# Norm sums: eight blocks of squares added on GpSimd, one matmul behind the low passes

## The reference, cut to what matters

```python
def rms_norm(x, g):
    y = x32 * lax.rsqrt(jnp.mean(x32 * x32, axis=-1, keepdims=True) + EPS)
    return (y * g.astype(jnp.float32)).astype(x.dtype)
...
        h = modulate(rms_norm(x, ln_ffn1[i]), sh1, sc1)
        x = x + 0.5 * g1[:, None, :] * swiglu(h, ffn1_wg[i], ffn1_wu[i], ffn1_wd[i])
        h = modulate(rms_norm(x, ln_mix[i]), sh2, sc2)
...
        x = x + g2[:, None, :] * mix
```

## Time and profile before

| what | value |
|---|---|
| runs shown | median 1736.61 us, 1735.37 to 1739.26, 3 runs |
| span of the profiled execution, first to last instruction | 1734.1 us |
| TensorE (PE) busy | 1708.0 us, 98% |
| VectorE (DVE) busy | 1412.9 us, 81% |
| ScalarE (ACT) busy | 908.4 us, 52% |
| GpSimd (POOL) busy | 435.0 us, 25% |
| mean granted clock of TensorE | 0.999 |

### The profile page before, as it was taken

The page is one execution under the profiler, slowest core; times in us unless marked ns, Lnnn a source line. Parts: engine busy times, 40 slices in busy tenths (PEclk is TensorE's granted clock), DMA queues, the critical chain, the costliest instruction groups (busy, mean ns, idle before and its releaser), DMA issues. The chain is left out here.

```text
span 1734.1 us, 36503 instructions
## 1 busy us (share of the span) xinstructions
PE 1708.0 (98%) x14039; PEld 1667.7 (96%) x14039; DVE 1412.9 (81%) x1924; ACT 908.4 (52%) x1274; POOL 435.0 (25%) x685
## 2 busy tenths in 40 slices
PE   7999999999999999999999999999999999999998
PEld 5999999999999999999999999999999998799998
DVE  6877898788778977898987799779988896788655
ACT  3443367764335533365634356667444567764444
POOL 6322321012223122321232224540322232401000
PEclk9999999999999999999999999999999999999999
DMA  9998858549887787867698865334988772257550
GB/s 338 356 359 279 294 178 280 166 158 321 304 304 242 276 302 270 302 212 272 229 314 305 302 199 191 115 132 156 322 297 293 230 199 83 78 199 251 184 176 25
DMA packets 261793, 411.45 MB, mean 237 GB/s; under 512 B 21950, under 2 KB 204414, under 8 KB 261560
## 3 DMA queue, kind: packets, MB, share of 16 engines
q1 hardware_dynamic: 224968, 290.67, 51.0%
q0 software_dynamic: 36720, 119.36, 19.4%
HBM read 408.90 MB, written 2.63 MB: 237 GB/s over the span
## 5 line engine op out<-in xcount | busy, mean ns | idle before, releaser
L2891 DVE TENSOR_TENSOR lo<-raw,hi 128x2048 fp32r<-128x2048 f32 (+2 forms) x251 | 565.6, 2256 | 162.4 <-ACT hi L2719 161.8
L2719 ACT CAST hi<-raw 128x2048 fp32r<-128x2048 f32 (+2 forms) x266 | 497.4, 1872 | 377.6 <-PE dacc L2388 189.4
L2386 PE MATMUL up<-operand_hi,hi 128*128 128x256 f32 x1952 | 553.1, 283 | 1.4 <-DVE lo L2891 1.4
L2387 PE MATMUL up<-operand_lo,hi 128*128 128x256 f32 x1952 | 552.3, 283 | 0.0
L2388 PE MATMUL up<-operand_hi,lo 128*128 128x256 f32 x1952 | 552.3, 283 | 0.0
L2163 POOL DMA_DIRECT2D ada<-in_ada_w_dram x448 | 267.3, 613 | 841.8 <-DVE ada_acc L2927 793.5
L2386 PEld LDWEIGHTS up<-operand_hi,hi 128*128 128x128 f32 x1952 | 374.4, 192 | 2.3 <-DVE lo L2891 2.0
L2388 PEld LDWEIGHTS up<-operand_hi,lo 128*128 128x128 f32 x1952 | 374.5, 192 | 0.0
L2387 PEld LDWEIGHTS up<-operand_lo,hi 128*128 128x128 f32 x1952 | 374.5, 192 | 0.0
L2927 DVE SCALAR_TENSOR_TENSOR ada_acc<-ada,c_col,ada_acc 128x512 f32<-128x512 f32 x420 | 315.3, 751 | 13.8 <-DMA ada<-in_ada_w_dram 0.6
L2386 PE MATMUL dacc<-act_hi,hi 128*128 128x256 f32 x976 | 276.2, 283 | 0.7 <-DVE act_lo L3103 0.7
(11 more groups left out here) (483 smaller groups left out, 2858.2 us busy)
## 6 DMA issues: line engine op xcount, KB each, us to landing
ada<-in_ada_w_dram POOLq DMA_DIRECT2D x448, 256.0 KB, 4.8
raw<-in_ffn_wg_dram SPq DMA_DIRECT2D x88, 512.0 KB, 5.4
raw<-in_ffn_wu_dram SPq DMA_DIRECT2D x88, 512.0 KB, 5.2
raw<-in_ffn_wd_dram SPq DMA_DIRECT2D x88, 512.0 KB, 5.6
raw<-in_ffn_w_up_dram SPq DMA_DIRECT2D x88, 512.0 KB, 4.6
raw<-in_ffn_w_down_dram SPq DMA_DIRECT2D x46, 512.0 KB, 4.6
raw<-in_hg_w_in_dram SPq DMA_DIRECT2D x32, 512.0 KB, 4.8
raw<-in_attn_w_qkv_dram SPq DMA_DIRECT2D x24, 512.0 KB, 7.7
```

Of the source, the lines that this page charges most:

```text
L2386: pe.matmul(o, stat[0], mov[0], start=start, stop=False, skip_group_check=True)
L2387: pe.matmul(o, stat[0], mov[1], start=False, stop=False, skip_group_check=True)
L2719: last = act.copy(put(slab(hi, s, SPL)), take(slab(raw, s, RAW)))
L2891: last = dve.tensor_tensor(put(slab(lo, s, SPL)), take(slab(raw, s, RAW)), put(slab(hi, s, SPL)).bitcast(F32), ALU.subtract)
```

## The change

In the seven phases GpSimd adds all eight blocks of squares (seven adds), TensorE sums the one block that is left, and it does so behind the low passes of the first slab instead of ahead of them. F0, the two gained phases and the last norm stay as they are.

```diff
             def pre_add(name):
...
-                acc, top, done = op_k(squares, 0), 5 if name in raw_first else 3, S["presummed"]
+                acc, top, done = op_k(squares, 0), KB - 1 if name in raw_first else 3, S["presummed"]
                 if name in gained:
                     acc, top, done = gain_acc, KB - 1, S["presummed_g"]
...
-                norm_sums(p)
+                if p in gained:
+                    norm_sums(p)
                 for k in range(KB):
                     pe.wait_ge(S["raw_lo_done"], KB * i + k + 1)
                     for h in range(2):
                         last = pe.matmul(dst[h], sl[0][:, k * SEQ + h * P:k * SEQ + (h + 1) * P], raw_k(raw_lo, k),
                                          start=False, stop=(k == KB - 1), skip_group_check=True)
                 last.then_inc(slab_used, 1)
+                if p not in gained:
+                    norm_sums(p)
                 slab_ready(b + 1)
...
-                order = list(range(KB)) if whole else [0, 6, 7] if name in raw_first else [4, 5, 0, 6, 7]
+                order = list(range(KB)) if whole else [0] if name in raw_first else [4, 5, 0, 6, 7]
```

## The result

The changed kernel takes 1742.91 us (median of 7 runs, 1741.78 to 1744.16), the kernel before 1737.59 us (7 runs, 1735.37 to 1739.26): ratio 1.0032, 95% interval 1.0021 to 1.0042, so 5.6 us slower (3.6 to 7.3). The forecast was 1741.8 us, 5.2 slower.

What follows compares the result with a forecast made beforehand. VectorE's chain to the fourth slab was taken to bound the seven phases. Losses of 0.80 + 0.71 + 0.61 + 0.24 + 3 x 0.95 = 5.2 us gave 1741.8 us; 8 in 10 range 1737.5 to 1747.

Steps and rivals of the forecast that it cites:

- The total: Whole kernel: 5.2 us slower, 1741.8 us from a median of 1736.61; the forecast had a chance of 0.56.
- VectorE, not TensorE, sets the fourth slab: Fourth slab of each phase: VectorE's split comes last; TensorE's saved 0.87 us a phase only lengthens its wait.
- Two adds cost VectorE 0.95 us a phase, read off F2: VectorE's last four low blocks: 3.12 us in F2 with seven adds, 2.17 in C1 with five; half split 0.95 later.
- The rival in which both adds block in full: VectorE stands still for both adds' whole 1.76 us a phase: 10.9 us slower, 1747.5 us; chance 0.03.
- The sum is not late: Behind the first slab's low passes: the one sum ends about 1538.4 in C1, covered by VectorE's splits, costing nothing.
- Slack of four phases, 5.2 us in all: TensorE's slack in A, F1, G, F3 cuts losses to 0.80, 0.71, 0.61, 0.24 us; C0, N, C1 lose 0.95 each.
- F3's slack of 0.71 us: Fourth slab of F3: TensorE started 0.71 us later than VectorE required, leaving a loss of 0.24 us.
- the hand-over: From VectorE's end to the waiting matmul's start: 0.06 us, C1's 0.05 rounded up, subtracted in each slack.
- Waits of 1 to 2 us at the fourth slab: TensorE would wait 1 to 2 us for VectorE's split in A, F1, F3, C0, N, C1; G for the scaled result.
- The clock: Rival: longer TensorE idles bring half-clock stretches; 1743 to 1745 us if in one or two phases, 1750 in five; chance 0.15.

Runs made afterwards that it cites:

- the move alone: Against the kernel before: five adds and three sums kept, but the sums stand behind the low passes; 1738.06 us, ratio 0.9999 (0.9989 to 1.0008).

## Why the prediction was right, step by step

- **The total.** 5.2 us slower was forecast, 5.6 measured. That 1741.8 stood against 1742.91 is in part the base: 1736.61 was the median of three runs, 1737.59 that of seven. And it was partly luck that the size came so near, since one term was about 1 us small (below).
- **VectorE, not TensorE, sets the fourth slab.** Right: with the sums taken off free of charge at most the slack came back (-1.0 us, -2.6 to +0.7), and with the sums given back the loss was the same (+5.2 for +5.6).
- **Two adds cost VectorE 0.95 us a phase, read off F2.** Right to 0.02: 3.14 us for the four blocks against the 3.12 of F2, half split 2.37 us behind the fifth add against 2.35. The rival in which both adds block in full, 1.76 us a phase, is answered by 0.49 us for each add: a block that meets an add does wait for its end (1543.21 against 1542.92 above), but only one block does so for each add, and the work of VectorE goes on in between.
- **The sum is not late.** Right: the move alone is 0.9999.
- **Slack of four phases, 5.2 us in all.** The mechanism was right, the term too small: 5.8 us by the trace, 6.3 with the clock alike. F3's slack of 0.71 us was read from an execution in which TensorE had been at half clock in F3, as the earlier trace rows show; without that it is 0.15 (0.21 less 0.06), the same as A's. That is 0.56 of the missing 1.1 us. The rest is mostly in the hand-over: the prediction let the waiting matmul start 0.06 us behind VectorE and counted nothing more. TensorE in A, the row behind the first matmul, in the changed kernel and then in the kernel before:
```profile
254.22 0.28 PE L2387 MATMUL misc<-operand_lo,hi 128*128 128x256 f32 x1
```
```profile
253.31 0.28 PE L2387 MATMUL misc<-operand_lo,hi 128*128 128x256 f32 x1
```
  Behind a first matmul that had to wait, the second starts 0.22 us later (254.00, 254.22), behind one that did not 0.12 (253.19, 253.31). So TensorE lost another 0.10 us in each of the four phases where it had not waited before, A, F1, G and F3; C0, N and C1 had paid it already. That is another 0.4 us. In the table it shows in the next phase's growth: F3's 0.10 is in C0's 1.05.
- **Waits of 1 to 2 us at the fourth slab.** Missed in part: C0 and C1 have 1.41 and 1.44, N 0.98, but A, F1 and F3 0.77 to 0.82, G 0.36. Some of the stall sits earlier, in a wait I had not seen: the second slab now comes to the half split too soon, as the row at 1545.28 shows (0.19 us). It costs nothing, being ahead of the wait that decides.
- **The clock.** No fall behind the new idles: from 10.30 to 1436.90 us, which takes in those of six phases, the granted clock is 1.00. The fall in N, which cost this execution 1.6 us, came after 13.90 us in which TensorE had no idle time. Rows of the move-alone run, which has no new idle either, show the same place:
```profile
1417.50:1431.30 13.80, 13.80 (x118) 13.60 (x116) 13.33 (x26) 7.18 (x15) 2.63 (x8) 1.00 1.02 216
1431.40:1438.10 6.70, 6.70 (x47) 6.53 (x48) 6.53 (x8) 1.71 (x2) 0.00 (x0) 0.50 0.82 190
```
  So the rival's mechanism is not what happened in the profiled execution; what starts such a stretch, no run here shows.

## What to carry to other kernels

A busy share of 98% does not say that an engine's work sets the end: ask, at the next wait behind the place, which engine comes last, and take the removed work as worth only that engine's slack. Moving an addition from TensorE to GpSimd is not free when VectorE runs instructions with two SBUF inputs beside it: count one held pass for each add, here 0.49 us for a 128x256 add, read from the same neighbours elsewhere in the trace, before counting what TensorE saves. Where both are tight, a cheaper form of the work on the engine that has it can beat handing it over: single-pass fp32r sums without any add gave 4.9 and 5.7 us here. And read a slack only where the clock was full: one of four here was mostly a stretch at half clock.

## What the runs showed of the hardware

- The hold-up is by add: 1.67 us for the four blocks with none or three adds, 2.17, 2.66 and 3.14 with five, six and seven. It is one block for each add that reaches into them: 0.96 us for 0.47, its end 0.29 us behind the end of the add (C1 of the changed kernel).
- The residual rows, which read PSUM and one SBUF input, were not held up: 0.86 us for two beside the adds, 0.88 in the run without any (the Trainium skill, "SBUF — State Buffer", section "Who interferes with whom", says that a VectorE instruction with at most one SBUF input, outside the 2-port performance modes, does not contend with GpSimd; these rows agree). So of the four chained adds of before, 3.32 us, VectorE pays only 1.04 in C1.
- Eight fp32r matmuls of 256 columns take 1.11 us as a group, six records of fp32 (three matmuls) 1.46.
- Behind a 256-column matmul that had to wait the next one starts 0.22 us later, in an unbroken row 0.12 (A, after and before): 0.10 us more than the wait itself.
